# A decoder step in one hand-ordered program: when the sampled pairs' key scores may start, and where the last exponentials of the fourth pair run

## The reference, cut to what matters

```
x = x + 1/2 * SwiGLU_1(RMSNorm(x))
h = RMSNorm(x); z = h @ w_in            # one combined projection
A: causal pooling, 4 groups x 64
B: 6 heads x 64, softmax attention: own block and the top 3 past blocks of 256 keys
C: 6 heads x 64, retention with decay
x = x + concat(A, B, C) @ w_out
x = x + 1/2 * SwiGLU_2(RMSNorm(x))
```

## Time and profile before

| | |
|---|---|
| runs | 1321.41, 1322.31, 1322.69 us; median 1322.31 us |
| profiled execution, its own time | 1318.97 us |
| span from first to last instruction | 1317.1 us |
| DVE busy | 787.9 us (60%) |
| ACT busy | 660.3 us (50%) |
| POOL busy | 237.3 us (18%) |
| transfers | 232.97 MB, mean 177 GB/s |
| mean granted TensorE clock | 0.995 |

### The profile page before, as it was taken

The page is one execution under the profiler, slowest core; times in us unless marked ns, Lnnn a source line. Parts: engine busy times, 40 slices in busy tenths (PEclk is TensorE's granted clock), DMA queues, the critical chain, the costliest instruction groups (busy, mean ns, idle before and its releaser), DMA issues.

```text
span 1317.1 us, 25155 instructions
## 1 busy us (share of the span) xinstructions
PE 1291.6 (98%) x9881; PEld 1243.8 (94%) x9881; DVE 787.9 (60%) x885; ACT 660.3 (50%) x838; POOL 237.3 (18%) x389
## 2 busy tenths in 40 slices
PE   9999999998999999999999999999899999999998
PEld 7999999997869999999999999999797799999998
DVE  6555555677876655554465555566877675555433
ACT  6555543345464655543365554333446455555433
POOL 1021000358541000000110000013855220000010
PEclk9999999999999999999999999999899999999999
DMA  6676544668994444444456554447599834444441
GB/s 202 203 199 193 167 140 153 187 171 209 284 343 156 136 159 149 138 152 144 151 166 187 165 183 145 150 150 202 142 253 311 292 128 160 144 143 159 144 148 68
DMA packets 201671, 232.97 MB, mean 177 GB/s; under 512 B 15006, under 2 KB 192936, under 8 KB 201604
## 3 DMA queue, kind: packets, MB, share of 16 engines
q1 hardware_dynamic: 194172, 209.10, 51.1%
q0 software_dynamic: 7312, 22.95, 5.9%
q10 hardware_dynamic: 120, 0.03, 0.0%
HBM read 226.83 MB, written 5.32 MB: 176 GB/s over the span
## 4 chain that ended last, share of the span: by engine, by line
PE 85%; DVE 6%; DMA 2%; ACT 2%; DVEq 2%; issue 1%; SPq 1%; ACTq 0%
PE ps L1477 24%; PE ps L1478 24%; PE ps L1479 24%; DMA kbuf<-in_cache_k 2%; PE ps L1597 2%; PE ps L1599 2%; PE ps L1598 2%; DVE w_lo L1024 1%; PE ps L1745 1%; SPq L410 1%; DVE kbuf L1143 1%; PE ps L1929 1%; ACT w_hi L702 1%; DVEq L1220 1%; PE ps L1931 1%
## 5 line engine op out<-in xcount | busy, mean ns | idle before, releaser
L702 ACT ACTIVATE w_hi<-w_raw 128x2048 fp32r<-128x2048 f32 x167 | 319.9, 1915 | 514.3 <-PE ps L1479 415.2
L1024 DVE TENSOR_TENSOR w_lo<-w_raw,w_hi 128x2048 fp32r<-128x2048 f32 x159 | 365.9, 2301 | 196.5 <-ACT w_hi L702 192.0
L1477 PE MATMUL ps<-h_hi,w_hi 128*128 128x320 f32 x768 | 237.9, 310 | 0.8 <-DVE h_lo L1112 0.7
L1479 PE MATMUL ps<-h_hi,w_lo 128*128 128x320 f32 x768 | 237.3, 309 | 0.0
L1478 PE MATMUL ps<-h_lo,w_hi 128*128 128x320 f32 x768 | 237.3, 309 | 0.0
L1477 PE MATMUL ps<-g_hi,w_hi 128*128 128x320 f32 x704 | 217.9, 309 | 0.0
L1479 PE MATMUL ps<-g_hi,w_lo 128*128 128x320 f32 x704 | 217.4, 309 | 0.0
L1478 PE MATMUL ps<-g_lo,w_hi 128*128 128x320 f32 x704 | 217.4, 309 | 0.0
L1478 PE MATMUL ps<-act_lo,w_hi 128*128 128x320 f32 x704 | 217.2, 309 | 0.0
L1477 PE MATMUL ps<-act_hi,w_hi 128*128 128x320 f32 x704 | 217.2, 309 | 0.0
L1479 PE MATMUL ps<-act_hi,w_lo 128*128 128x320 f32 x704 | 217.2, 309 | 0.0
(11 more groups left out here) (309 smaller groups left out, 1764.0 us busy)
## 6 DMA issues: line engine op xcount, KB each, us to landing
w_raw<-in_ffn_w_in SPq DMA_DIRECT2D x87, 1024.0 KB, 5.1
w_raw<-in_ffn_w_out SPq DMA_DIRECT2D x32, 896.0 KB, 4.6
w_raw<-in_w_in SPq DMA_DIRECT2D x22, 1024.0 KB, 5.4
kbuf<-in_cache_k SPq DMA_DIRECT2D x96, 192.0 KB, 5.1
w_raw<-in_ffn_w_out SPq DMA_DIRECT2D x16, 1024.0 KB, 4.9
w_raw<-in_w_out SPq DMA_DIRECT2D x8, 1024.0 KB, 7.0
kbuf<-in_cache_k POOLq DMA_DIRECT2D x32, 192.0 KB, 3.7
kbuf<-in_cache_v SPq DMA_DIRECT2D x32, 192.0 KB, 5.1
```

Source lines behind the costliest of these rows:

```text
L702: act.activation(w_hi[:, slot, :], w_raw[:, slot, :], ACT.Copy).then_inc(hi_done, 1)
L1024: dve.tensor_tensor(w_lo[:, slot, :], w_raw[:, slot, :], w_hi[:, slot, :].bitcast(F32), ALU.subtract).then_inc(split_done, 1)
L1477: pe.matmul(out, w_hi[:, slot, w], hi[:, k, :], start=(k == 0), stop=False)
L1479: ins = pe.matmul(out, w_lo[:, slot, w], hi[:, k, :], start=False, stop=(k == k_all - 1))
```

## The change

Three things change in each layer.

1. PE drops four waits: `scores(0)` no longer waits for `sm_in` of pair 0, and `sample_scores(1)`, `(2)` and `(3)` no longer wait for `s_max`. `sample_scores(p)` still waits for its turned keys, its query copies and `sm_in` of the pair before. DVE turns the last piece of pair 1's keys before `mix_lo(6)`, not after it.
2. `sample_scores(2)` moves from ahead of `mix(9)` to between its halves; on DVE `evac_first(9)` goes ahead of `soft_in(2)`.
3. On ACT, `exps(3)` is split 2 + 7 and no longer 4 + 5, and the seven stand behind `vr_tokens`, ahead of `pool_hi`.

```diff
-                exps(3, range(4))
+                exps(3, range(2))
                 out_evac(0)
                 act.wait_ge(stored_va, 16 * (L + 1))
                 att_evac(2)
-                exps(3, range(4, 9))
                 for t in range(3):
                     vr_tokens(t)
+                exps(3, range(2, 9))
...
                 turn_k(1, 1, 0)
+                turn_k(1, 1, 1)
                 mix_lo(6)
-                turn_k(1, 1, 1)
...
+                evac_first(9)
                 soft_in(2)
-                evac_first(9)
                 soft_bias(2)
...
-                pe.wait_ge(sm_in, L * 4 + 1)
                 scores(0)
...
-                pe.wait_ge(s_max, H * L + 2)
                 sample_scores(1)
...
-                pe.wait_ge(s_max, H * L + 4)
+                mix(9, (0,))
                 sample_scores(2)
-                mix(9)
+                mix(9, (1,))
...
-                pe.wait_ge(s_max, H * L + 6)
                 sample_scores(3)
```

## The result

| | before | after |
|---|---|---|
| median of the runs | 1321.86 us (6 runs) | 1332.35 us (6 runs, 1327.78 to 1333.79) |
| ratio | | 1.0080, 95% interval 1.0061 to 1.0099 |
| profiled execution / span | 1318.97 / 1317.1 us | 1331.74 / 1330.1 us |
| mean granted TensorE clock | 0.995 | 0.990 |
| DVE busy | 787.9 us | 797.8 us |

The forecast was 1324.4 us, with a range up to 1328. The sign was right, the size was not: +2.1 us was worked out, 10.5 us came (12.8 between the two profiled executions).

The account below looks back on a forecast made before the run. PE, busy 98% of the span, bounds the kernel, with DVE's chain limiting gains; +1.7 - 0.4 + 0.8 = +2.1 us took 1318.97 to 1321.1, and 3.34 us to the median gave 1324.4 us, range 1319.5 to 1328.

Parts of the forecast that it names:

- parts 1 and 2, layer 0: At transpose_p(5) and all behind it in layer 0: past_ok 1.0 us later plus 0.7 for the clock, +1.7 us.
- parts 1 and 2, layer 1: At transpose_p(5) and all behind it in layer 1: past_ok 1.1 us earlier, plus 0.7 for the clock, -0.4 us.
- exponentials, both layers: Seven exponentials ahead of pool_hi start ret_out(0) 0.4 us later in each layer; +0.8 us over two layers.
- several stops on L1154: Before chunks 6 to 8, PE gives back its gain in stops of 0.3 to 1.2 us.
- DVE does not speed up: Behind pair 1's earlier scores, DVE's chain keeps its pace, so of 4.65 us won only 1.1 is left at mix(8).
- my middle value: At soft_bias(2), POOL's two mix_lo(11) pieces were to add 1.5 us, between bounds of 0 and 2.0.
- The clock behind past_ok: After PE's 3.4 us stop at past_ok, a clock fall priced at 1.7 us, of which 0.7 delays transpose_p(5).
- slower outright: Rival at past_ok: both POOL pieces hit, 3.9 us stop, low clock takes 2.6; +4.9 us, 1327.2; chance 0.28.
- any other case: Remaining rivals: DVE's chain clean, 1320.0 (0.14); stops really go, down to 1306 (0.04); change does nothing, 1322.3 (0.04).

Follow-up runs that it names:

- parts 1 and 2: The change without its third part (exponentials stay split 4 + 5), against the kernel before: 1327.24 us, ratio 1.0050.
- The run with one wait on POOL: Kernel before plus the change's first part, with POOL starting chunk 8's low part only after soft_bias(1): 1315.03 us, ratio 0.9962.
- part 3 alone: Kernel before with only the 2 + 7 split of pair 3's exponentials, the seven ahead of pool_hi: 1323.88 us, ratio 1.0029.
- the late exponentials alone: Kernel before with only pair 3's exponentials split 2 + 7, the seven behind att_high: 1317.33 us, ratio 0.9976.
- part 2 alone: Kernel before with only pair 2's scores between the halves of mix(9) and evac_first(9) ahead of soft_in(2): 1326.17 us, ratio 1.0046.
- the last version with part 2: The change with the seven exponentials behind att_high and POOL waiting for bias chains before chunks 8 and 11: 1316.75 us, ratio 0.9979.
- the changed kernel with POOL's waits: The change plus POOL waiting for the second bias chain before mix_lo(8) and the third before mix_lo(11): 1326.96 us, ratio 1.0061.

## Why the prediction was wrong

| step | worked out | measured |
|---|---|---|
| parts 1 and 2, layer 0 | +1.7 | +2.1 |
| parts 1 and 2, layer 1 | -0.4 | +5.1 |
| exponentials, both layers | +0.8 | +5.8 |
| sum, on the profiled executions | +2.1 | +13.0 |

(All at L1819 of the profiled executions. Rows 1 and 2 are parts 1 and 2 less before, row 3 is after less parts 1 and 2, in both layers. In the medians parts 1 and 2 are +6.6 us and the exponentials +3.9, so the profiled pair overstates the third row.)

**What held.** DVE's chain bounds this stretch, not the dropped waits; PE's gain is given back in several stops on L1154. Pair 2's own scores end at 334.9 (334.8 worked out) and soft_in(2) starts at 335.0 (334.9). PE arrives at past_ok at 345.0 (344.7) and stands 3.73 us (3.4). POOL's low part of chunk 11 blocks soft_bias(2), and PE begins mix(8) in layer 0 at 319.95, as worked out. ret_out(0) waits for L1380, with no wait at L1896.

**What failed, by size.**

*The layer 1 term, -0.4: wrong by 5.5 us, half of the miss.* The step that failed is "DVE does not speed up", taken for both layers as if no other engine did, with the chain's length kept but for chunk 11's low part. I went through POOL for chunks 10 and 11 only. The earlier scores of pair 1 free POOL, whose copies had waited 2.09 us for them in layer 1, and ACT's rounding behind mix(6). POOL's low part of chunk 8 then falls on soft_bias(1): 3.7 us on DVE, a stop of 3.71 us and a low clock on PE. The chain, now late, is blocked for another 3.9 us in q_dec (chunk 10) and for 2.0 in soft_bias(2) (chunk 11), of which the prediction had 1.5. The rows were in the trace of before; I did not look at who else waited for the event that the change brings forward. The run with one wait on POOL (part 1 from +2.9 to -5.0 us, layer 1 9.4 us shorter) shows this as the cause.

*The exponentials, +0.8: wrong by 5.0 us in the profiled pair, by 3 in the medians.* The term was the delay of ret_out(0) alone, 0.4 us a layer. The delay measured 1.0 us (layer 0 of part 3 alone), and the stop in front of it 2.1 to 2.3 us, which is over the 1.68 us of the earlier trace rows. By the same reasoning that gave past_ok a price for the clock this stop should have had one, and got none. Moving the seven behind att_high takes the stop away and gives 5.0 us of the change back.

*Parts 1 and 2, layer 0: wrong by 0.4 us.* The chain from soft_in(2) to past_ok took 13.6 us (335.02 to 348.64) where 13.2 were worked out. POOL's two pieces both hit: 1.25 and 1.18 us where such instructions take 0.19, 2.1 us added and not 1.5. Here the rule of the Trainium skill (SBUF — State Buffer, "Who interferes with whom"), by which both pieces block, was the better guide than my middle value:

```profile
340.80 1.25 DVE L1246 TENSOR_TENSOR ss<-ss 128x32 f32<-128x32 f32 x1
342.12 1.18 DVE L1248 SCALAR_TENSOR_TENSOR ss<-ss 128x32 f32<-128x32 f32 x1
343.38 0.23 DVE L1250 TENSOR_REDUCE ss<-ss 128x8 f32<-128x40 f32 x1
```

(DVE's timeline of the kernel after.) The clock behind past_ok was priced at 1.7 us, of which 0.7 was to come through. In the kernel after PE needs 8.2 us from L1766 to head 5's transposes, 2.3 more than its 5.95 us of work, and 1.3 come through (8.26 us behind past_ok, 6.97 before).

The rival "slower outright" named the right place, past_ok, at 4.9 us. It would have been exceeded too: neither it nor any other case held the block on soft_bias(1), and none gave the exponentials a low clock.

**Still open:** why POOL's two waits gain only 2.5 us while the seven exponentials stand ahead of pool_hi, and 8.3 when they do not; why part 3 costs 3.8 us in the median; and what the late exponentials alone gain beyond the 1.4 us expected.

## What to carry to other kernels

When an event is brought forward, list everyone who waited for it, on every engine, and follow each to the instructions it will now run beside; the engine that bounds may be slowed by one that had been waiting. A late engine off the critical path can be worth keeping late: one wait on POOL was worth 7.9 us here. Price each new stop of PE with the clock behind it, and move small work of ACT behind the operation that PE waits for, not ahead of it.

## What the runs showed of the hardware

In these runs the clock behind a stop can't be read from the length of the stop. In part 2 alone PE stood 3.73 us before past_ok in both layers. In layer 0 the clock stayed at its full level, 2.4 GHz, in layer 1 it fell to 1.2 GHz. The stretches of that kernel, behind either stop:

```profile
349.00:351.00 2.00, 1.15 (x10) 1.11 (x11) 1.87 (x6) 0.02 (x1) 1.50 (x3) 1.00 0.95 217
...
1000.00:1002.00 2.00, 2.00 (x10) 2.00 (x9) 1.76 (x6) 1.48 (x6) 1.27 (x4) 0.50 0.95 278
```

Shorter stops went both ways too. In layer 0, 2.18 us before past_ok had a low clock behind it in the last version with part 2 (0.53 in the stretch shown there) and none in the changed kernel with POOL's waits (1.00 from 347 to 353 us). In part 3 alone 2.12 us before ret_out(0) had it in layer 0 and not in layer 1. The 1.68 us of the earlier trace rows had none. So a stop of 2 to 4 us was a chance of a fall here; prices in the prediction that rest on one stop each were thinner than they looked.

A row of small products pays for one POOL piece after the other. The six of q_dec (L1342, both inputs in SBUF) stood beside the four pieces of chunk 10's low part (985.26 to 990.30 us) in layer 1 of the kernel after: 4.86 us, against 1.00 in the kernel before. The two key turns behind soft_bias(2), beside two such pieces in layer 0 of the kernel before, took 3.42 us, no longer than elsewhere.

```profile
985.80 4.86 DVE L1342 TENSOR_TENSOR q_dec<-z,q_decay 64x64 f32<-64x64 f32 x6
```
